# Norm's weights over 128 rows at the start of a two-layer trunk: a load on another queue, two more dummies, one moved part of the bias's rows

## The reference

```python
def rmsnorm(x, w):
    xf = x.astype(jnp.float32)
    y = xf * lax.rsqrt(jnp.mean(xf * xf, axis=-1, keepdims=True) + NORM_EPS)
    return (y * w.astype(jnp.float32)).astype(x.dtype)

for l in range(DEPTH):
    h = rmsnorm(x, norm_w[l])
    proj = h @ w_in
    ...                      # k, w/a, r, v of RWKV-7 first; MoBA adds bias_tab[t5_bucket(q_pos - k_pos)]
    x = x + y @ w_out
return rmsnorm(x, final_norm_w)
```

## Time and profile before

| what | value |
|---|---|
| three runs, median | 575.93 us (575.54 to 576.25) |
| the profiled execution | 576.12 us |
| its span | 574.3 us |
| TensorE matmul busy | 565.8 us |
| VectorE, ScalarE, GpSimd busy | 379.9, 277.8, 249.5 us |
| waits of TensorE that the trace names, in all | 2.5 us |

### The profile page before, as it was taken

The page is one execution under the profiler, slowest core; times in us unless marked ns, Lnnn a source line. Parts: engine busy times, 40 slices in busy tenths (PEclk is TensorE's granted clock), DMA queues, the critical chain, the costliest instruction groups (busy, mean ns, idle before and its releaser), DMA issues. The chain is left out here.

```text
span 574.3 us, 12717 instructions
## 1 busy us (share of the span) xinstructions
PE 565.8 (99%) x5230; PEld 461.7 (80%) x5230; DVE 379.9 (66%) x644; ACT 277.8 (48%) x555; POOL 249.5 (43%) x197
## 2 busy tenths in 40 slices
PE   8999999999999999999999999999999999999995
PEld 6978888888877777888898788888888777788884
DVE  4989986482488557774444897947436865778173
ACT  6486241343574474534657643324357335735253
POOL 4937552044941322536335455402386313145340
PEclk9999999999999999999999999999999999999999
DMA  9546634056432122354544433332743321224513
GB/s 281 160 125 204 218 99 111 9 130 149 107 81 75 39 75 72 100 180 130 162 123 134 111 78 107 89 69 59 163 128 80 79 71 39 73 75 147 181 43 143
DMA packets 103374, 64.58 MB, mean 112 GB/s; under 512 B 29152, under 2 KB 94228, under 8 KB 103317
## 3 DMA queue, kind: packets, MB, share of 16 engines
q1 hardware_dynamic: 103316, 63.77, 39.9%
HBM read 55.61 MB, written 8.14 MB: 111 GB/s over the span
## 5 line engine op out<-in xcount | busy, mean ns | idle before, releaser
L706 POOL TENSOR_TENSOR w_lo<-w_raw,w_hi 128x512 fp32r<-128x512 f32 x156 | 216.7, 1408 | 282.2 <-ACT w_hi L1307 280.7
L770 PE MATMUL bank<-act_hi,w_hi 128*128 128x512 f32 x432 | 173.2, 401 | 0.0
L773 PE MATMUL bank<-act_lo,w_hi 128*128 128x512 f32 x432 | 168.5, 390 | 0.0
L772 PE MATMUL bank<-act_hi,w_lo 128*128 128x512 f32 x416 | 162.3, 390 | 0.0
L1307 ACT ACTIVATE w_hi<-w_raw 128x512 fp32r<-128x512 f32 x140 | 80.2, 621 | 78.3 <-PE bank L869 28.2
L770 PEld LDWEIGHTS bank<-act_hi,w_hi 128*128 128x128 f32 x432 | 81.1, 188 | 24.8 <-issue 8.4
L773 PEld LDWEIGHTS bank<-act_lo,w_hi 128*128 128x128 f32 x432 | 81.1, 188 | 17.4
L772 PEld LDWEIGHTS bank<-act_hi,w_lo 128*128 128x128 f32 x416 | 78.2, 188 | 14.9
L1233 PE MATMUL bank<-w_hi,act_hi 128*128 128x512 f32 x128 | 50.0, 391 | 0.0
L1235 PE MATMUL bank<-w_hi,act_lo 128*128 128x512 f32 x128 | 49.8, 389 | 0.0
L1234 PE MATMUL bank<-w_lo,act_hi 128*128 128x512 f32 x128 | 49.8, 389 | 0.0
(11 more groups left out here) (223 smaller groups left out, 946.2 us busy)
## 6 DMA issues: line engine op xcount, KB each, us to landing
w_raw<-in_w_in_dram SPq DMA_DIRECT2D x62, 512.0 KB, 4.0
w_raw<-in_w_out_dram SPq DMA_DIRECT2D x16, 512.0 KB, 3.8
pages<-in_x_dram SPq DMA_DIRECT2D x4, 512.0 KB, 6.2
x_or_y<-in_x_dram SPq DMA_DIRECT2D x4, 512.0 KB, 3.9
x_scratch<-x_or_y SPq DMA_DIRECT2D x4, 512.0 KB, 3.1
x_or_y<-x_scratch SPq DMA_DIRECT2D x4, 512.0 KB, 3.7
out_dram<-pages SPq DMA_DIRECT2D x8, 256.0 KB, 2.2
bias_scratch<-pages SPq DMA_DIRECT2D x1, 1280.0 KB, 7.5
```

Source lines behind the costliest of these rows:

```text
L706: ins = pool.tensor_tensor(low, raw, w_hi[:, i % HI, k, 0:n].bitcast(F32), ALU.subtract)
L770: mm(b[:, :], hi, act_hi[:, k, :], start=n == 0, stop=False)
L772: mm(b[:, :], lo, act_hi[:, k, :], start=False, stop=False)
L773: ins = mm(b[:, :], hi, act_lo[:, k, :], start=False, stop=n == KT - 1)
```

## The change

The norm's row goes to partition 0 of a page whose other 127 rows are zero. GpSimd clears the page's second half and VectorE its first half (semaphore `norm_clear`), and ScalarE, as its first act, waits for both and issues the load. The two products that spread it have 128 rows of ones instead of one. SyncE's first issue is now x's block 0. TensorE runs six dummies instead of four. Of the bias's rows, part 1 is made behind the shift of r0 and no longer behind that of k1; it is now the last, and raises `bias_rows`.

```diff
-        norm_row = page(10)[0:1]
+        norm_rows = page(10)
@@ SyncE
-            load(norm_row, norm_w[0:1, :], "norm_loaded")
@@ GpSimd
                 pool.memset(to, value).then_inc(s("units"), 1)
+            pool.memset(norm_rows[:, T:2 * T], 0.0).then_inc(s("norm_clear"), 1)
             pool.memset(par_rows, 0.0).then_inc(s("par_clear"), 1)
@@ TensorE
-            idle(4)
+            idle(6)
             pe.wait_ge(s("units"), 1)
             pe.wait_ge(s("norm_loaded"), 16)
             for a in range(2):
                 b = begin(f"nw{a}", -1)
-                end(mm(b[:, :], one[0:1, :].to_broadcast([1, P]), norm_row[:, a * T:(a + 1) * T], start=True, stop=True), f"nw{a}", -1)
+                end(mm(b[:, :], one.to_broadcast([P, P]), norm_rows[:, a * T:(a + 1) * T], start=True, stop=True), f"nw{a}", -1)
@@ ScalarE
             go = act.activation
+            act.wait_ge(s("norm_clear"), 2)
+            act.dma_start(norm_rows[0:1], norm_w[0:1, :]).then_inc(s("norm_loaded"), 16)
             act.wait_ge(s("units"), 3)
@@ VectorE
+            dve.memset(norm_rows[:, 0:T], 0.0).then_inc(s("norm_clear"), 1)
             dve.memset(bias_rows[:, :, T:DIST], MASKED)
@@ VectorE, bias_runs
-                if part == 3:
+                if part == 1:
                     ins.then_inc(s("bias_rows"), 1)
@@ VectorE, shift
-                    if layer == 0 and job in ("k0", "k1"):
-                        bias_runs(int(job[1]))
+                    if layer == 0 and job in ("k0", "r0"):
+                        bias_runs(0 if job == "k0" else 1)
```

## The result

The changed kernel takes 577.5 us at the median of its runs (576.14 to 578.0); the kernel before, run beside it, 575.99 us (575.27 to 576.78). The ratio is 1.002, with an interval of 1.001 to 1.0029: slower by 1.5 us where I forecast 0.6 us less, and outside my range. The profiled execution of after took 576.83 us, with a span of 575.0 us; that of before 576.12 us and 574.3 us.

A forecast was written before the change was run, and what follows sets the result against it. TensorE's products were busy 99% of the span, so only the prologue could gain: 0.6 us kept, the bias move at 0, 575.93 - 0.6 = 575.3 us (own range 575.0 to 575.7); overall range 574.7 to 577.2 us.

The forecast's parts named there:

- the row's landing: Prologue, norm row issued by ScalarE at 1.6 us: there at 4.4 us, between 3.9 and 6.4 us.
- line 748 past 5.5 us: Sign that the forecast is wrong: the products spreading the norm's row, expected at 4.4 us, start after 5.5 us.
- the hole: TensorE's idleness between the end of the six dummies at 3.6 us and the row's products: 0.8 us.
- My sum: Row's products from 4.4 us: nw1 ends at 7.8 us at the low clock, 7.0 us if it has risen.
- my first rival: Prologue: row held among x's packets, landing at 6 us or later; 577.2 us, or 577.9 us with clock low; chance 0.20.
- x first: SyncE's queue without the row's issue: x's block 0 0.40 us earlier, at 4.63 us, GpSimd's first split at 8.19 us.
- The new work of ScalarE and GpSimd: Prologue: memset of 0.48 us, row issued at 1.6 us, table load behind it; costs ScalarE nothing under 1.1 us.
- The clock: TensorE in the prologue: 128-row work raises the clock by 8 us, so transposes stand 0.11 us apart, not 0.21 us.
- the rival's figure for a low clock: Late row with the clock low: fourth high part at 13.3 us, 2.0 us late, 577.9 us.
- The chain to `kk_square`: Fourth high part to `kk_square` through GpSimd's splits and v0's load: TensorE keeps 0.6 us, between 0.2 and 0.9 us.
- The moved part: Bias copies of 0.66 to 0.70 us behind r0's shift: cost 0, absorbed by line 1732's hold-off; other end 0.70 us.

The follow-up runs named there:

- the four built on before: The kernel before with the move alone (575.91 us), x first alone (575.42 us), that plus x's block 2 issued earlier (575.57 us), or two more dummies (576.52 us).

## Why the prediction was wrong

**The step that failed: the row's landing.** I took 4.4 us, near the lower end of 3.9 to 6.4 us, "since it is 4 KB and the nearest row is that of the same load". It was used at 5.59 us, 4.06 us after its issue where I had allowed 2.8 us, and at 5.56 to 5.95 us in the six other kernels that issue it behind x. My own sign of being wrong, "line 748 past 5.5 us", came. It is small, but size was the wrong property: most of the time went by before its packet started, not in moving it. The same 4 KB issued at 1.53 us with nothing ahead of it was used from 3.71 us. The nearer row was that of x's second block, also issued while the first was under way, which gave the upper end.

The late row alone is not the whole loss. With ten dummies it was used as late, at 5.77 us, and the median was that of before, 576.07 us: 0.8 us of the forecast is gone, and no more. The rest came where the row's products, behind the hole, still ran at the lower level: nw1 took until the first transposes at 9.14 us, where with ten dummies these started at 7.99 us. My sum had both levels for these products, but with the row at 4.4 us, where VectorE would have waited for nw1 about 1 us at most (8.1 against 7.03 us).

This is my first rival: "It decides from a landing at about 5.2 us on". Its places are borne out. It had VectorE's second multiplication at 9.65 us and the fourth high part at 12.6 us; they came at 9.39 and 12.40 us. It had the first transposes behind nw1; they are, at 9.14 us. I gave it 0.20.

The sentence from the Trainium skill that I set beside the sum, "DMA: Bandwidth & Descriptors", section "Issuing engines are not separate DMA queues", says that loads of different issuers interleave on the same 16 engines and that only issue time is saved. The trace agrees in so far as the second queue bought the row no way past an x that was issued ahead of it. It shows little interleaving: 0.86 MB of SyncE's packets were served before the row's single one. Issued 0.8 us behind x, the row's products started 2.6 us later than in the earlier trace rows, for 0.4 us of x's.

**x first: right.** Forecast 4.63 us for x and 8.19 us for GpSimd's first split; the trace has 4.61 and 8.04 us. Done alone the step is worth 0.56 us at the median, where 0.4 us was expected of it.

**The new work of ScalarE and GpSimd: right.** The memset took 0.53 us against 0.48 us, the issue began at 1.53 us against 1.6 us, and the table load behind it delays nothing: ScalarE idles another 1.06 us before x.

**The clock: right in direction, wrong in time.** I held a rise by 8 us likelier than not. In the profiled execution it came between 9.14 and 10.19 us, too late for the products, in time for the transposes, which ran 0.11 us apart from 10.19 us on. With a clock still low the second multiplication's delay would have cost more; the fourth high part is 1.09 us late and not 2.0 us, the rival's figure for a low clock. My reason, work of 128 rows, is shown by the pair with ten dummies for holding the clock once it is up: 0.50 after one-row products, 1.00 after 128 rows, 1.1 us between them. For raising it there are only the profiled executions with six dummies and no hole, high behind 128 rows (two of the kernel with x held back) and low behind one row (before with six dummies). But the hole was 1.7 us, not the 0.8 us of my sum, because the row was late. Executions of kernels with that hole then fell on both sides: products of 0.9 us in after, its repetition and the kernel with four dummies, of half of that in two others (one-row products, move undone). The Trainium skill has in "TensorE: Matmul & The Clock Gate", section "What's actually happening", that the number of slow products at a kernel's start varies from run to run; these traces agree, as TensorE's program up to the products is the same in after, its repetition and the kernel with the move undone.

**The chain to `kk_square`: right.** I wrote that the delay or gain of the fourth high part passes through k1's split, r0's split and the load of v0 to `kk_square`. The starts in the profiled executions (us; the fourth high part, GpSimd's split behind k1's high part, `kk_square`, and how long the third comes after the first; in before, with ten dummies and 128 rows, and with x first alone the row was used straight behind the dummies, so it may have landed earlier):

| kernel | row used | 4th high part | GpSimd | `kk_square` | after the high part |
|---|---|---|---|---|---|
| before | 3.00 | 11.31 | 13.87 | 35.13 | 23.8 |
| after | 5.59 | 12.40 | 14.96 | 36.00 | 23.6 |
| after again | 5.81 | 12.61 | 15.17 | 36.25 | 23.6 |
| after, four dummies | 5.56 | 12.06 | 14.62 | 35.61 | 23.6 |
| after, one-row products | 5.90 | 11.60 | 14.16 | 35.04 | 23.4 |
| after, ten dummies | 5.77 | 10.89 | 13.44 | 34.64 | 23.8 |
| ten dummies, one-row | 5.95 | 11.74 | 14.29 | 35.41 | 23.7 |
| after, move undone | 5.68 | 10.69 | 13.24 | 34.26 | 23.6 |
| x first alone | 3.20 | 10.32 | 13.66 | 34.71 | 24.4 |

In the eight kernels above the last, GpSimd starts 2.55 or 2.56 us behind the fourth high part, and `kk_square` 23.4 to 23.8 us behind it. The last is the exception that the chain explains: there x's block 2 is what ScalarE waits for. In after the steps between are late too: r0's split ends at 26.13 us against 25.07 us, v0's load is there at 30.22 us against 29.36 us.

**The moved part: right, and by the reason given.** In after the copies and the multiplication behind them are:

```profile
40.80 0.69 DVE L1678 COPY pages<-pages 128x24 f32<-128x24 f32 x8
...
45.25 1.24 DVE L1734 SCALAR_TENSOR_TENSOR pages<-pages,params 128x512 f32<-128x512 f32 x1
...
69.99 0.67 DVE L1791 SCALAR_TENSOR_TENSOR x_or_y<-x_or_y,bank 128x512 f32<-128x512 f32 x1
```

GpSimd's split that the multiplication starts in, in before and in after:

```profile
43.78 1.30 POOL L706 TENSOR_TENSOR w_lo<-w_raw,w_hi 128x512 fp32r<-128x512 f32 x1
```
```profile
44.63 1.30 POOL L705 TENSOR_TENSOR w_lo<-w_raw,w_hi 128x512 fp32r<-128x512 f32 x1
```

Before, after and the move alone (split 43.43 to 44.73 us) agree: the multiplication ends 0.55 us behind the end of that split, at 45.63, 46.49 and 45.27 us, wherever in it it started. Against the earlier trace rows the multiplication starts 1.49 us late and ends 0.86 us late; the shift of r0 ahead of the copies, at 40.14 us, was 0.87 us late, so the copies have vanished. The read of g1 is 0.61 us late, less than TensorE's 0.87 us at `kk_square`, and rq1 has no wait. Undoing the move in after, and making it alone, changes the time by less than can be told.

**The size.** The trace of after is 0.7 us longer than that of before, and the rival had it at 1.3 us for a fourth high part at 12.6 us. The medians lie 1.5 us apart. In part the profiled execution was simply a short one: its own kernel's median is 0.67 us above it. What is behind the rest can be bounded by taking the start of `kk_square` from the time of each profiled execution. For before, after, after with one row, with ten dummies, and the four built on before this leaves 540.7 to 541.1 us. For the other six, all built on after, it leaves 541.2 to 542.5 us: TensorE stood still later on, in five of them with an idle time that the trace puts down to no one. Two of those, of the one with ten dummies and one row (waits), and of the repetition of after (timeline):

```profile
PE bank L1002 <- issue: 0.7, 1, 0.7
PE bank L772 <- issue: 0.6, 1, 0.6
```
```profile
132.22 0.33 PE L1058 MATMUL bank<-pages 64*64 64x64 f32 x3 [0.45 <-issue]
```

Such stalls may be what after's median has on top of 0.87 us. Nothing here shows what makes them, nor that the change does: the kernel before and the four built on it show no such idle time in their one profiled execution each, and four of after's family show none either, after's own among them. That part of the loss stays open.

## What to carry to other kernels

A small load that something waits for is best issued ahead of or beside the first big one (on another queue, but 0.8 us later, it stood 3 us behind 0.86 MB), and its landing is to be priced by a row of a load issued under the same traffic, not by the same load alone. Work that is to warm TensorE's clock should last until the latest landing of what comes next: with a hole of 1.7 us and more the level at the products differed between executions, and closing it took 1.4 us off the median. Of this change's parts the one that helped by itself (x first, 0.56 us) was undone by what was put around it: clearing 127 rows put the row's load 0.8 us behind x's.

## What the runs showed of the hardware

- A packet of 4 KB on ScalarE's queue, issued 0.8 us behind the first of two 512 KB loads on SyncE's queue, started over 3.1 us after its issue; issued without that lead, it was through in under 1.3 us.
- Products of one row at the high level (records of 0.59 us, 0.43 us from start to start) were followed by a granted clock of 0.50, in one kernel from 8 to 10 us, where TensorE was busy the whole time; products of 128 rows with the same columns were followed by 1.00.
- The granted clock's column reads 1.00 until the first change on record, also in stretches where starts and durations show the low level (after's products at 5.59 us, 0.9 us each, in the window below). At a kernel's start the pace has to be read from the starts.

```profile
6.00:8.00 2.00, 2.00 (x3) 0.74 (x3) 0.41 (x2) 1.42 (x4) 0.00 (x0) 1.00 1.10 390
```

- A VectorE multiplication that waits out a GpSimd split is the same one in 1.87 and in 1.25 us: work put in front of it cost nothing for as long as that wait lasted. It ended 0.55 us behind the end of the split in three kernels.
